# Stationary blocks read with a step of two, moving operand and output walked backward

## The reference

```python
z, xbc, dt_raw, q_a, c_kv, k_rope, gate_ssd, gate_mla = split_cols(u @ w_in[i], IN_SPLITS)
y_ssd = ssd_branch(...) @ w_ssd_out[i]
y_mla = mla_branch(...) @ w_mla_out[i]
merged = jax.nn.sigmoid(gate_ssd) * y_ssd + jax.nn.sigmoid(gate_mla) * y_mla
h = h + merged @ w_o[i]
h = h + memory_cross_attention(...)
h = h + hierarchical_moe(...)
...
```

## Time and profile before

| | us |
|---|---|
| median of 3 runs | 1050.41 |
| lowest and highest of them | 1043.98, 1050.57 |
| profiled execution, its own time | 1049.15 |
| its span, first to last instruction | 1047.3 |
| TensorE matmul busy, of the span | 992.2 (8,552 instructions) |
| weight loads busy | 916.9 |
| VectorE busy | 626.5 |
| ScalarE busy | 514.5 |

### The profile page before, as it was taken

The page is one execution under the profiler, slowest core; times in us unless marked ns, Lnnn a source line. Parts: engine busy times, 40 slices in busy tenths (PEclk is TensorE's granted clock), DMA queues, the critical chain, the costliest instruction groups (busy, mean ns, idle before and its releaser), DMA issues.

```text
span 1047.3 us, 19394 instructions
## 1 busy us (share of the span) xinstructions
PE 992.2 (95%) x8552; PEld 916.9 (88%) x8552; DVE 626.5 (60%) x836; ACT 514.5 (49%) x695; POOL 19.6 (2%) x23
## 2 busy tenths in 40 slices
PE   7999999999999999999996678699999999999998
PEld 6999999899989999997673456499999999999998
DVE  6798789868676875452111010289975765555566
ACT  5576597844675563533110111277566653343453
POOL 0000021001000000000000000000000000000000
PEclk9999999999999999999998899899999999999999
DMA  7665453446246367889999999955323355555531
GB/s 290 246 237 191 172 201 124 165 159 237 82 141 213 135 236 281 317 353 384 419 421 421 420 421 420 377 207 176 121 81 138 119 201 201 197 187 187 190 122 41
DMA packets 34871, 241.74 MB, mean 231 GB/s; under 512 B 4064, under 2 KB 4448, under 8 KB 6368
## 3 DMA queue, kind: packets, MB, share of 16 engines
q1 hardware_dynamic: 33264, 233.32, 58.8%
q0 software_dynamic: 1232, 6.99, 1.9%
q10 hardware_dynamic: 288, 0.15, 0.1%
HBM read 239.36 MB, written 1.08 MB: 230 GB/s over the span
## 4 chain that ended last, share of the span: by engine, by line
PE 76%; DMA 12%; DVE 7%; ACT 2%; SPq 2%; issue 1%; DVEq 0%; ACTq 0%
PE ps L482 18%; PE ps L484 18%; PE ps L483 18%; DMA wr<-in_c_weights 8%; PE ps L571 3%; PE ps L1292 3%; DMA T8b<-in_c_weights 3%; SPq L3090 2%; DVE wlo L2063 2%; PE ps L979 1%; PE ps L1242 1%; DVE xs L2295 1%; ACT whi L1402 1%; PE ps L1319 1%; PE ps L855 1%
## 5 line engine op out<-in xcount | busy, mean ns | idle before, releaser
L2063 DVE TENSOR_TENSOR wlo<-raw,whi 128x2048 fp32r<-128x2048 f32 (+1 forms) x119 | 271.0, 2280 | 113.4 <-ACT whi L1402 113.0
L482 PE MATMUL ps<-XUh,whi 128*128 128x256 f32 x992 | 280.9, 283 | 0.7 <-DVE wlo L2063 0.6
L483 PE MATMUL ps<-XUl,whi 128*128 128x256 f32 x992 | 276.7, 279 | 0.0
L484 PE MATMUL ps<-XUh,wlo 128*128 128x256 f32 x992 | 276.7, 279 | 0.0
L1402 ACT ACTIVATE whi<-raw 128x2048 fp32r<-128x2048 f32 (+1 forms) x119 | 225.0, 1893 | 48.1 <-PE ps L484 41.2
L482 PEld LDWEIGHTS ps<-XUh,whi 128*128 128x128 f32 x992 | 186.9, 188 | 2.7 <-issue 1.7
L483 PEld LDWEIGHTS ps<-XUl,whi 128*128 128x128 f32 x992 | 188.0, 190 | 0.7 <-issue 0.5
L484 PEld LDWEIGHTS ps<-XUh,wlo 128*128 128x128 f32 x992 | 186.3, 188 | 0.0
L3013 DVE SCALAR_TENSOR_TENSOR sphs<-sphs,wsl,ps 128x256 f32<-128x256 f32 x8 | 3.8, 480 | 89.7 <-ACT sphs L2028 71.4
L484 PE MATMUL ps<-ffnah,wlo 128*128 128x256 f32 x176 | 49.5, 281 | 0.0
L482 PE MATMUL ps<-ffnah,whi 128*128 128x256 f32 x176 | 49.5, 281 | 0.0
(11 more groups left out here) (633 smaller groups left out, 2365.8 us busy)
## 6 DMA issues: line engine op xcount, KB each, us to landing
raw<-in_c_weights SPq DMA_DIRECT2D x137, 1024.0 KB, 4.9
wr<-in_c_weights SPq DMA_DIRECT2D x36, 1024.0 KB, 26.1
xhi<-in_c_weights SPq DMA_DIRECT2D x12, 1024.0 KB, 26.3
xlo<-in_c_weights SPq DMA_DIRECT2D x12, 1024.0 KB, 26.4
extra<-in_c_weights SPq DMA_DIRECT2D x10, 1024.0 KB, 27.5
T<-in_c_weights SPq DMA_DIRECT2D x5, 1024.0 KB, 26.1
T8b<-in_c_weights SPq DMA_DIRECT2D x5, 1024.0 KB, 26.4
acb<-sums POOLq DMA_DIRECT2D x4, 1024.0 KB, 5.0
```

The costliest lines, as they stand in the source:

```text
L482: pe.matmul(ps, h(k), xh(k), start=start and k == 0, stop=False, skip_group_check=loose)
L483: pe.matmul(ps, h(k), xl(k), start=False, stop=False, skip_group_check=loose)
L484: t = pe.matmul(ps, l(k), xh(k), start=False, stop=stop and k == kt - 1, skip_group_check=loose)
L2063: dve.tensor_tensor(l[:, 0:n], r, h[:, 0:n].bitcast(F32), ALU.subtract).then_inc(*did("w_lo", "split", i))
```

## The change

The host reorders the columns of every split piece whose weights are stationary (`braided`): two neighbouring blocks of 128 columns are interleaved, column 0 of the first, column 0 of the second, column 1 of the first, and so on. A new view `blocks_of` picks block b of a piece as every second value, so that a stationary operand's 128 columns lie 8 bytes apart where they lay 4 bytes apart. The blocks are counted through the k-tiles: block `2 * k + j` for pieces of 256 columns, `8 * k + d` for pieces of 1,024. Pieces that are not split, those of the experts and those of `chunk_tok` stay as they were; of `kv_b` only the key half is braided.

A new helper `backward` turns an operand's last dimension round: it starts at the last value and steps by -1. `triple_back` is `triple` with the moving operand and the output both turned. Position n of the activation still lands in position n of the output, but both are walked from 255 to 0. The splitting on ACT and DVE, the loads, the number and order of the instructions and every wait stay as they were.

```diff
+def braided(name, count, a):
+    kept = {"dt": 9, "lora": 9, "xv": 9, "hv": 9, "sv": 9, "e_gate": 99, "e_up": 99, "e_down": 99,
+            "hz": 1, "w_out2": 1, "f_gate": 1, "ple_gate": 1}
+    if count < kept.get(name, 0):
+        return a
+    if name == "kv_b":
+        x = a.reshape(128, 2, 8, 128)
+        y = x[:, :, 0:4].reshape(128, 2, 2, 2, 128).transpose(0, 1, 2, 4, 3).reshape(128, 2, 4, 128)
+        return np.concatenate([y, x[:, :, 4:8]], axis=2).reshape(128, -1)
+    return a.reshape(128, -1, 2, 128).transpose(0, 1, 3, 2).reshape(128, -1)
...
+    def blocks_of(i):
+        n = pieces[i][1] * pieces[i][2]
+        def block(x, b):
+            return x[slot_of(i)][:, 0:n].rearrange("p (q m t) -> p q t m", m=128, t=2)[:, b // 2, b % 2, :]
+        return tuple(lambda b, x=x: block(x, b) for x in (hi, lo))
...
+    def backward(x):
+        a = list(x.ap)
+        step, n = a[-1]
+        return bass.AP(x.tensor, x.offset + step * (n - 1), a[:-1] + [[-step, n]])
...
+        def triple_back(ps, h, l, xh, xl, kt, ready=None, start=True, stop=True, loose=False):
+            return triple(backward(ps), h, l, lambda k: backward(xh(k)), lambda k: backward(xl(k)), kt, ready, start, stop, loose)
...
         def chunk(name, c, xh, xl, kt, ready, nt=2, ...):
-            h, l = split_of(i)
+            h, l = blocks_of(i)
...
-                t = triple(ps[:, 256 * j:256 * j + 256], lambda k: h[:, k, 128 * j:128 * j + 128], lambda k: l[:, k, 128 * j:128 * j + 128],
+                t = triple_back(ps[:, 256 * j:256 * j + 256], lambda k: h(nt * k + j), lambda k: l(nt * k + j),
                            lambda k: xh[:, k, :], lambda k: xl[:, k, :], kt, ready)
```

More of the change, by code:

```diff
@@ L1 @@
+import collections
 import itertools
@@ L230, in weights @@
     several("ple_gate", I["ple_gate_2"][0], 0, 1024)
+    seen = collections.Counter()
+    for i, (name, kt, a) in enumerate(parts):
+        parts[i] = name, kt, braided(name, seen[name], a)
+        seen[name] += 1
     return parts
@@ L523, in chunks_late @@
                     for j in range(2):
-                        d, f = pss[c][:, 256 * j:256 * j + 256], slice(128 * j, 128 * j + 128)
+                        d = backward(pss[c][:, 256 * j:256 * j + 256])
                         for k in part:
                             w.wait_ge(*ready(k))
-                            pe.matmul(d, h[:, k, f], xh[:, k, :], start=k == j == 0, stop=False, skip_group_check=True)
-                            pe.matmul(d, h[:, k, f], xl[:, k, :], start=False, stop=False, skip_group_check=True)
-                            t = pe.matmul(d, l[:, k, f], xh[:, k, :], start=False, stop=k == kt - 1, skip_group_check=True)
+                            pe.matmul(d, h(2 * k + j), backward(xh[:, k, :]), start=k == j == 0, stop=False, skip_group_check=True)
+                            pe.matmul(d, h(2 * k + j), backward(xl[:, k, :]), start=False, stop=False, skip_group_check=True)
+                            t = pe.matmul(d, l(2 * k + j), backward(xh[:, k, :]), start=False, stop=k == kt - 1, skip_group_check=True)
                     if kt - 1 in part:
@@ L711, in pe_program @@
                 for j in range(2):
-                    f = slice(256 * r + 128 * j, 256 * r + 128 * j + 128)
-                    t = triple(ps[:, 256 * j:256 * j + 256], lambda k: h[:, k, f], lambda k: l[:, k, f],
+                    b = 2 * r + j
+                    t = triple_back(ps[:, 256 * j:256 * j + 256], lambda k: h(4 * k + b), lambda k: l(4 * k + b),
                                lambda k: XCh[:, k, :], lambda k: XCl[:, k, :], 3)
@@ L720, in pe_program @@
             h, l = split_of(i)
+            hb_, lb_ = blocks_of(i)
             w.wait_ge(*at_("n_ckv", "lo", 0))
@@ L726, in pe_program @@
                 for j in range(2):
-                    a = 4 * r + 2 * j
-                    t = triple(ps[:, 256 * j:256 * j + 256], lambda k: h[:, k, 64 * a:64 * a + 128], lambda k: l[:, k, 64 * a:64 * a + 128],
+                    b = 2 * r + j
+                    t = triple_back(ps[:, 256 * j:256 * j + 256], lambda k: hb_(8 * k + b), lambda k: lb_(8 * k + b),
                                lambda k: XCh[:, 3 + k, :], lambda k: XCl[:, 3 + k, :], 2)
@@ L865, in pe_program @@
             w.wait_ge(*free)
-            t = triple(ps[:, 0:256], lambda k: h[:, k, 128 * j:128 * j + 128], lambda k: l[:, k, 128 * j:128 * j + 128],
+            t = triple_back(ps[:, 0:256], lambda k: h(2 * k + j), lambda k: l(2 * k + j),
                        lambda k: OXh[:, k, :], lambda k: OXl[:, k, :], 8)
@@ L1102, in ffn_up @@
             for j in range(2):
-                t = triple(ps[:, 256 * j:256 * j + 256], lambda k: h[:, k, 128 * j:128 * j + 128], lambda k: l[:, k, 128 * j:128 * j + 128],
+                t = triple_back(ps[:, 256 * j:256 * j + 256], lambda k: h(2 * k + j), lambda k: l(2 * k + j),
                            lambda k: XUh[:, k, :], lambda k: XUl[:, k, :], 8, ready)
@@ L1115, in ffn_down @@
                 ps = yb[d // 2][0][:, 256 * (d % 2):256 * (d % 2) + 256]
-                t = triple(ps, lambda k: h[:, k, 128 * d:128 * d + 128], lambda k: l[:, k, 128 * d:128 * d + 128],
+                t = triple_back(ps, lambda k: h(8 * k + d), lambda k: l(8 * k + d),
                            lambda k: fah[c % 2][:, k, :], lambda k: fal[c % 2][:, k, :], 2, start=c == 0 and d % 2 == 0, stop=c == 10, loose=True)
@@ L1142, in ple_proj @@
             for j in range(2):
-                d = slice(256 * q + 128 * j, 256 * q + 128 * j + 128)
-                t = triple(ps[:, 256 * j:256 * j + 256], lambda k: h[:, k, d], lambda k: l[:, k, d], lambda k: PTh[:, k, :], lambda k: PTl[:, k, :], 2)
+                b = 2 * q + j
+                t = triple_back(ps[:, 256 * j:256 * j + 256], lambda k: h(8 * k + b), lambda k: l(8 * k + b), lambda k: PTh[:, k, :], lambda k: PTl[:, k, :], 2)
             if q < 3:
```

## The result

The changed kernel took 1,059.6 us (median of 4 runs, 1,059.1 to 1,059.9) against 1,047.2 us for the kernel before (four runs, two near 1,043.7 and two near 1,050.5, so that the median lies between them). The ratio is 1.0125, 95% interval 1.0087 to 1.0163: slower, by 0.9 to 1.6%, where 0.52 stood on faster. By the prediction's own bounds of 1,040 and 1,061 us this is its "same", with a chance of 0.26. The time lies at the upper edge of the range of 1,014 to 1,060.

A forecast was written before the change was run, and what follows sets the result against it. TensorE, 76% of the chain, bounds the kernel through its triples; 9.3 us feed-forward, 1.2 first projection and 12.1 elsewhere make 22.6, times 0.89 is 20, from 1,049.15 to 1,029, with the transfers' lead 1,028 us; range 1,014 to 1,060.

The forecast's parts named there:

- What bounds the kernel, and how the sum is made: Whole kernel: TensorE's triples lead; only their pace moves the time; 5,232 changed matmuls gain 22.6 us, 20 us arriving.
- 0.89 was taken: Share of the triples' gain reaching the end, 76/85, from TensorE's 76% of the chain against VectorE and ScalarE's 9%.
- The case of every triple at 113.4 ns: All changed triples settle at the faster existing pace: 13.3 us gained, 11.8 after the factor, 1,037 us.
- The 1 us that it added for an earlier start of the experts' transfers: Experts' stretch: an earlier first block frees buffers and gives transfers a small lead, 1,029 to 1,028 us.
- The yardstick: Plain float32 products, 128 columns at 109.1 and 111.6 ns; float32r's excess of 2 to 9 ns is winnable by reading order.
- Walking backward, "I take 111.6 ns": Changed triples: load and stream pass in opposite directions, less in each other's way; pace 111.6 ns, lower bound 109.1.
- The step of two, "I take nothing": Weight loads of changed triples: reading every second value costs nothing, as loads are not the longer part now.
- Rival "nothing happens": Changed triples: address order doesn't set the two paces; 1,049 us, or 1,058 if all fall to 117.7 ns; chance 0.26.
- its sign: For the rival that nothing happens: the changed profile still shows both paces of the triples.
- Rival "walking backward halves the stream": Changed matmuls: falling order handles values one by one, pace 215.9 ns, 523 us slower, 1,572 us; chance 0.12.
- Rival "the load is the bound": Changed triples: the stepped load sets the pace, about 205 ns at twice the time, 1,519 us; chance 0.10.
- VectorE late between 160 and 204 us: Around attention and norms: VectorE, busy 38.70 of 44.00 us, is late next where triples shorten; TensorE's waits for it grow.

The follow-up runs named there:

- the last version: The kernel before with lb (128 bytes) placed between the whi and wlo tiles, so wlo lies 128 bytes further on: 1,040.2 us, ratio 0.9941.
- the bare products: Kernels without the computation: sections of 96 float32r products, no other engine at work, varying step, direction, tile distance and preceding instructions; 113.3 to 120.8 ns a product.

## Why the prediction was wrong

*What bounds the kernel, and how the sum is made*: right. The pace of the triples carried the difference. Of the 11.4 us that 2.17 ns x 5,232 make, 10.8 - 1.4 = 9.4 us reached the end, a share of 0.82 where 0.89 was taken. The case of every triple at 113.4 ns, priced at 1,037 us, came in the last version: 113.6 ns and 1,040.2 us. But the sum began at 1,049.15 us, an execution with the feed-forward layer in its slower state, and the 6.6 us that it saw to be won there at 113.4 ns are what the kernel before wins by itself in half of its ten runs. The 1 us that it added for an earlier start of the experts' transfers no run shows; in the last version a lead shrank there.

*The yardstick* was read wrongly. Plain products with full loads run at 109 to 112 ns, and the prediction took the excess of the float32r products over them for something that a different order of reading gives back. No float32r products of 256 columns settled under 113.3 ns (to 0.1 ns) in any run, and the kernel before already ran at that pace in part of its time, by the place of its tiles.

*Walking backward, "I take 111.6 ns"*: the step that failed. Alone it took every triple to 117.8 ns. The argument was one of speeds: load and stream pass each other faster and are less in each other's way. That would help at every distance. Measured, the backward walk is 1.6 ns faster at a distance of 0 and 4.5 ns slower at the kernel's 192: the pace goes by the remainder of the tiles' distance modulo 256 bytes, the direction and the step together. That the pace hangs on load and stream together was right. That the time still lies in the range is luck as far as the forecast goes; the range took in the upper end of a rival. The Trainium skill, "TensorE: Matmul & The Clock Gate", in the section on the steps of a matmul, has the weight load take no read bandwidth from the running matmul. By that rule the place of the tiles should not matter; 64 bytes of padding turn 113.3 and 117.8 into 120.0 ns for float32r, and the measurement decides.

*The step of two, "I take nothing"*: mis-sized. Alone it costs 120.0 - 115.6 = 4.4 ns a product; the load's record grows by 5 to 7 ns in the kernel. The Trainium skill, "SBUF — State Buffer", in the section on the DMA port swizzle, calls two reads in a 16-byte line enough for full speed. At a distance of 0 this agrees (120.0 ns with either step), at 192 forward it doesn't (113.3 against 120.0).

*Rival "nothing happens"*: its upper end, all triples at 117.7 ns and 1,058 us, is what came, though not its sign, both paces still there. Its price was right, its chance too small, and its reason wrong. "Both paces occur with the same addresses, so addresses alone don't choose between them" missed that addresses can decide which paces exist, and the entry which of them is taken. Had the earlier trace rows been read so, a change of every address pattern would have put the fast pace itself at risk, since the earlier trace rows show it in the first projection and in most of a piece of `kv_b`, and that case would have deserved the largest chance.

*Rival "walking backward halves the stream"*: did not come. The output's direction is worth nothing in the bare products (within 0.1 ns). The rule of the Trainium skill, "PSUM — Partial Sum Buffer", Specifications, on access that is not contiguous does not extend to a falling walk over neighbouring values.

*Rival "the load is the bound"*: did not come. The loads' records are 5 to 7 ns longer with the step, but at 117.8 ns the changed kernel has the pace that the backward walk has with loads of 188 ns.

*VectorE late between 160 and 204 us*: the change couldn't test it, since the triples got no shorter. In the last version they are shorter there, 114.0 ns where the prediction's profile has 115.3, and TensorE's waits for VectorE in that stretch are 2.3 us, as before.

**Open**: what in the memory has the period of 256 bytes, why a state once entered lasts for over 1,500 matmuls, what tips the feed-forward layer into one or the other, and why `wlo` 128 bytes further helps. The runs show the dependence, not the part of the chip that makes it.

## What to carry to other kernels

When identical instructions show two paces in one trace, look for what makes the faster one possible before changing any address, and price its loss as a case of its own. For float32r products with a new load each, the place of the moving tile against the stationary one modulo 256 bytes is a setting worth 6% of the product's time; it costs a few bytes of padding to try, and where the entry doesn't decide, the bare products predicted the whole kernel's mean to 0.3 ns a product. Two groups of runs a few microseconds apart can be one such state taken or missed, so profile one of each.

## What the runs showed of the hardware

- A float32r product of 128x128 by 256 columns, step one and forward, took 113.3, 117.8, 118.7 or 120.0 ns by the distance of its moving tile from its weights modulo 256 bytes, with no other engine at work.
- At a distance of 192 bytes it had two lasting states, 113.3 and 117.8 ns. With no other engine at work what ran just before chose between them; in the kernel the same instructions led to either. With `wlo` 128 bytes further only the first lasted, after all four entries.
- The output's direction in PSUM made no difference (118.3 and 118.3, 120.0 and 120.0 ns).
- Loads with a step of two had records of 193 to 198 ns against 188 to 192.
